# One step of a gated-conv and mixture-of-experts decoder on one core: one expert's load, the tiles' last order, and a second load queue

## The reference, cut to what matters

```python
x = x + jnp.concatenate([z_a, z_b], axis=-1) @ w_out
x = x + _hier_moe(_rmsnorm(x, g_ffn), ...)     # the top 2 of 8 experts in the best of 4 groups
...
for e in range(N_EXPERTS):                      # 32
    hid = jax.nn.silu(t @ w_gate[e]) * (t @ w_up[e])
    out = out + combine[:, e:e + 1] * (hid @ w_down[e])
...
y_prompt = _rmsnorm(xp, g_final)
y_sample = _rmsnorm(xs, g_final)
```

## Time and profile before

| what | us |
|---|---|
| median of 3 runs (lowest, highest) | 535.75 (534.46, 538.24) |
| the profiled execution, its own time | 540.91 |
| its span | 539.0 |
| TensorE busy | 483.3 (90%) |
| VectorE, ScalarE, GpSimd busy | 237.7, 100.4, 183.3 |
| DMA | 141.25 MB, mean 262 GB/s |
| chain that ended last: TensorE, DMA, VectorE, issue, SP's queue | 71%, 12%, 5%, 5%, 3% |

### The profile page before, as it was taken

How to read it: one execution, slowest core, us unless ns; L and a number is a source line. 1 busy time by engine, 2 the same in 40 slices (tenths; PEclk the granted TensorE clock), 3 DMA queues, 4 the chain that set the end, 5 groups by cost and what they waited for, 6 DMA issues and landing times.

```text
span 539.0 us, 8928 instructions
## 1 busy us (share of the span) xinstructions
PE 483.3 (90%) x3301; PEld 285.3 (53%) x3302; DVE 237.7 (44%) x514; ACT 100.4 (19%) x204; POOL 183.3 (34%) x282
## 2 busy tenths in 40 slices
PE   6999999999999999999679998989898982998884
PEld 3787777777777545545334443444443441443331
DVE  4219999999964422245821222222122210221246
ACT  5131011002104423324301111101111110011223
POOL 3010817647394600111234443333443332234101
PEclk9989999999999999999789999999999996999999
DMA  8995006100000597023959799999999999999477
GB/s 328 310 391 142 0 2 258 54 2 0 1 1 1 189 412 315 39 69 124 403 192 420 284 411 422 402 397 421 419 418 419 417 419 420 420 418 421 195 272 256
DMA packets 35509, 141.25 MB, mean 262 GB/s; under 512 B 10080, under 2 KB 10096, under 8 KB 23193
## 3 DMA queue, kind: packets, MB, share of 16 engines
q1 hardware_dynamic: 29194, 127.91, 60.4%
q0 software_dynamic: 4960, 9.45, 4.7%
q10 hardware_dynamic: 1327, 3.49, 1.8%
HBM read 134.47 MB, written 13.17 MB: 274 GB/s over the span
## 4 chain that ended last, share of the span: by engine, by line
PE 71%; DMA 12%; DVE 5%; issue 5%; SPq 3%; ACT 2%; POOL 1%; DVEq 0%; POOLq 0%; ACTq 0%
PE bank L1284 26%; PE bank L1367 10%; PE bank L1485 9%; PE bank L1505 8%; PE bank L1480 8%; DMA region_x<-in_w_up 5%; DMA region_w<-in_w_in 3%; PE bank L1277 2%; DMA slot<-y_rows 2%; SPq L402 2%; PE bank L1495 2%; PE bank L1433 1%; DVE ua L1169 1%; PE bank L1393 1%; DVE ua L1171 1%
## 5 line engine op out<-in xcount | busy, mean ns | idle before, releaser
L1284 PE MATMUL bank<-region_h,region_w 128*128 128x256 f32 (+1 forms) x576 | 142.3, 409 | 0.0
L1284 PEld LDWEIGHTS bank<-region_h,region_w 128*128 128x128 f32 x576 | 110.2, 192 | 30.5 <-issue 0.8
L1169 DVE TENSOR_TENSOR ua<-ua,bank 128x128 f32<-128x128 f32 x30 | 8.7, 288 | 174.2 <-ACT ua L639 174.2
L1367 PE MATMUL bank<-region_w,z 128*128 128x512 f32 x128 | 56.7, 596 | 0.2 <-ACT z L584 0.2
L1505 PE MATMUL bank<-region_w,ua 128*32 128x512 f32 x328 | 50.3, 598 | 3.3 <-DVE ua L1171 3.3
L928 DVE SCALAR_TENSOR_TENSOR z<-ub,par,z 128x512 f32<-128x512 f32 x60 | 48.7, 812 | 0.0
L928 DVE SCALAR_TENSOR_TENSOR region_x<-ub,par,region_x 128x512 f32<-128x512 f32 x56 | 45.9, 820 | 0.0
L1485 PE MATMUL bank<-region_w,z 128*32 128x256 f32 x512 | 45.1, 403 | 0.2 <-issue 0.2
L792 POOL COPY gcol<-gidx 128x1 uint32 (+1 forms) x30 | 5.4, 180 | 108.9 <-DVE sb_rows L1158 108.9
L723 POOL TENSOR_TENSOR ub<-region_x 128x512 f32<-128x512 f32 x4 | 20.2, 5056 | 63.8 <-ACT ub L538 32.6
L1485 PE MATMUL bank<-slot,z 128*32 128x256 f32 x192 | 25.9, 425 | 14.5 <-DMA region_w<-in_w_up 9.9
(11 more groups left out here) (244 smaller groups left out, 647.5 us busy)
## 6 DMA issues: line engine op xcount, KB each, us to landing
region_w<-in_w_down SPq DMA_DIRECT2D x21, 1024.0 KB
region_w<-in_w_gate SPq DMA_DIRECT2D x16, 1024.0 KB
region_w<-in_w_up SPq DMA_DIRECT2D x16, 1024.0 KB, 15.7
region_w<-in_w_in SPq DMA_DIRECT2D x4, 2048.0 KB, 19.5
slot<-in_w_gate SPq DMA_DIRECT2D x6, 1024.0 KB, 14.8
slot<-in_w_up SPq DMA_DIRECT2D x6, 1024.0 KB
slot<-in_w_down SPq DMA_DIRECT2D x6, 1024.0 KB
region_x<-in_w_up SPq DMA_DIRECT2D x5, 1024.0 KB
```

The costliest lines, as they stand in the source:

```text
L1284: ins = mm(ps[2 * bank + j][:, 0:LEN[j]], sec[name][:, k, c * P:(c + 1) * P], hT[:, k, CUT[j]], start=(k == 0), stop=(k == KC - 1))
L1367: ins = mm(ps[2 * (t % 2) + j][0:n, :], z[:, k, t * P:t * P + n], w_out_sb[:, k, j * 512:(j + 1) * 512], start=(k == order[0]), stop=(k == ...
```

## The change

Three edits. Place 4's three loads move from behind the wait for the normalized rows to behind the first gather (SP's wait for those rows moves along), ahead of place 5's last part. The order in which tiles are finished changes from 0, 2, 1, 4, 3 to 0, 4, 2, 1, 3: loads, additions, norms, roots and stores follow, and the counts of the waits with them (`SUMMED` is 0, 4, 2). And the y of k = 1 of tiles 0 and 1 (`BY_ACT`) is loaded from ScalarE's queue, behind waits of its own for the last scatters and one small activation; SP issues the other eight.

```diff
+BY_ACT = (0, 1)
-FINISH = (0, 2, 1, 4, 3)
+FINISH = (0, 4, 2, 1, 3)
+SUMMED = tuple(t for t in FINISH if t not in BY_PE)
...
             load_expert(3, 3)
-            sp.wait_ge(s_h2, NT)
-            load_part(4, 0, 4)
-            load_part(4, 1, 4)
-            load_part(4, 2, 4)
             for i in range(2):
                 sp.wait_ge(s_h2d[i], 16 * ((NT + 1 - i) // 2))
             sp.wait_ge(s_x1t, 2 * NT)
+            sp.wait_ge(s_h2, NT)
             sp.wait_ge(s_gath[0], 16)
+            load_expert(4, 4)
             load_part(5, 0, 5)
             sp.wait_ge(s_tab, 1)
...
-            for t, k in ((0, 0), (0, 1), (2, 0), (1, 0), (2, 1), (1, 1), (4, 0), (4, 1), (3, 0), (3, 1)):
+            for t, k in ((0, 0), (4, 0), (4, 1), (1, 0), (2, 0), (2, 1), (3, 0), (3, 1)):
                 sp.dma_start(yg[k][t][0:TROWS[t], :], y_dram[k * NTOK + t * P:k * NTOK + t * P + TROWS[t], :])\
                   .then_inc(s_yg[k][t], 16)
...
+            act.wait_ge(s_ysc[1], pairs * 16)
+            act.wait_ge(s_ysc[0], (pairs + odd) * 16)
+            nc.scalar.activation(small[:, 63:64], eps_rms, ACT.Sqrt)
+            for t in BY_ACT:
+                act.dma_start(yg[1][t][:, :], y_dram[NTOK + t * P:NTOK + (t + 1) * P, :]).then_inc(s_yg[1][t], 16)
             for at, t in enumerate(FINISH):
...
-                act.wait_ge(s_fin, t // 2 + 1)
+                act.wait_ge(s_fin, SUMMED.index(t) + 1)
...
-                    dve.wait_ge(s_fin1, t // 2 + 1)
+                    dve.wait_ge(s_fin1, SUMMED.index(t) + 1)
...
             add_row(0, 0)
             add_row(0, 1)
+            add_row(4, 0)
+            normed(0)
+            add_row(4, 1)
             add_row(2, 0)
-            normed(0)
+            normed(4)
             add_row(2, 1)
-            add_row(4, 0)
-            normed(2)
-            add_row(4, 1)
-            for t in (1, 4, 3):
+            for t in (2, 1, 3):
                 normed(t)
```

## The result

The changed kernel took 542.18 us (median of 4 runs, 539.76 to 543.01) against 535.9 of before (4 runs, 534.46 to 538.24, three of them those shown above): a ratio of 1.0078, 95% interval 1.0047 to 1.011. (Ratios here are worked out from all the runs, and differ a little from the quotient of the two medians, which is 1.012 in this case.) Forecast were 535.0 and a range up to 538.7, so the forecast was wrong, and on the wrong side. Two repeats, each with 12 runs beside 35 of before, gave 1.0024 (0.9998 to 1.005) and 1.0005 (0.9976 to 1.0034).

What follows compares the result with a forecast made beforehand. From 306 us the expert weight stream was taken to set the pace, then the tail after the last scatter. Stream -2.4 plus tail +1.7 gave -0.7: 540.91 to 540.2, less the carried 5.2, 535.0 us; range 532.0 to 538.7.

Steps and rivals of the forecast that it cites:

- I take 3.0: First gather with idle engines: takes 3.0 us instead of 4.77, so it lands 1.8 us earlier.
- I expect the clock not to drop: TensorE's first block: fillers lead straight into it, so its first 62 matmuls take 3.87 us instead of 5.23, 1.4 more gained.
- TensorE leads by 3.2 us after its first block: Start of the blocks: the earlier gather (1.8) and the kept clock (1.4) put TensorE 3.2 us ahead.
- the lesser of 2.4 and TensorE's lead: Weight stream: moved loads fill idle engine time, reaching the state of 306 us 2.4 us earlier; gain taken as 2.4.
- I carry the difference over: Total: the profiled execution ran 5.2 us above the runs' median, and the forecast subtracts the same 5.2 from 540.2.
- rival B: Gather isn't helped or the lead is lost in the stream, while ScalarE's order costs 1.7 us: 537.45, chance 0.2.
- part 1: Place 4's matrices loaded behind the first gather: gain 2.4 us, bounds nothing to 2.9.
- I cost the second queue at zero: Tail y loads: a second queue only saves issue time, 5 us of issue against 16 us to the last landing; effect zero.
- ScalarE's row of three tiles takes the place of the last landing as the bound: Tail: ScalarE works through tiles 2, 1 and 3 in a row, making the tail 1.7 us longer.
- A: Rival: the tail is free, through earlier landings for tile 2 or a short GpSimd operation: 533.3, chance 0.15.
- C: Rival: tile 4's half-speed packets slow the other queue's full tiles beside them, 1.05 us on top: 536.1, chance 0.1.
- D: Rival: interleaving is no hindrance, other ports stay filled, 1 MB moves at 420, 1.05 us less: 534.0, chance 0.1.

Runs made afterwards that it cites:

- b0: The kernel before, unchanged, run and profiled again: 537.78 us, ratio 0.9995 to before.
- a0: The changed kernel run again without any diff: ratio 1.0024 to before.
- p1_move: Before with only the move of place 4's three loads behind the first gather: ratio 0.9983 to before.
- d1: The changed kernel without the second queue, all ten y loads on SP in order 0, 4, 1, 2, 3: ratio 0.9975 to before.
- p2_order: Before with only the tile order changed to 0, 4, 2, 1, 3, all ten y loads on SP: ratio 1.0005 to before.
- a1: The changed kernel with 50 instead of 32 fillers ahead of tile 1's first y: ratio 1.001 to before.
- p3_queue: Before, in its own tile order, with only the second y of tiles 0 and 1 loaded from ScalarE's queue: ratio 1.0016 to before.
- c1_t1first: a1 with tile 1 finished ahead of tile 2 (order 0, 4, 1, 2, 3), same loads: ratio 0.9999 to before.
- d0: The changed kernel run once more without any diff, in the last session: ratio 1.0005 to before.
- a2: The changed kernel with tile 1's first y issued second on SP's queue instead of fourth: ratio 1.004 to before.
- d3: Before with only place 4's down matrix moved behind the first gather, keeping 24 fillers: ratio 0.9968 to before.
- c4_split18: Before with only place 4's down matrix moved behind the first gather, and 18 instead of 24 fillers: ratio 0.9972 to before.

## Why the prediction was wrong

**The gather and the clock: right as read, wrong as a gain.** "I take 3.0" for the gather: measured 3.1, and 2.99 to 3.66 in all nine other profiles with all three loads moved, against 4.1 to 4.9 in the five profiles that moved none. "I expect the clock not to drop": so it was, 3.87 us. But in b0 the clock doesn't drop either, and the chain goes through fillers that end 5.2 us after the gather's issue. The step that failed is "TensorE leads by 3.2 us after its first block". Against b0 the lead is 0.1 us (5.62 to 5.70), and 1.2 where the fillers run at the upper clock (4.53 in a0). It was a lead over the one execution of before, among five, whose fillers were short (5.35 us) and ran out ahead of the gather.

**The stream: the arithmetic held, and the lesser of two terms was wrong.** The rule was "the lesser of 2.4 and TensorE's lead". With the lead at about 0 the gain is about 0, and p1_move measures 0.9983 (0.995 to 1.0016), no change that can be told from none. I had computed the lead from the profile of before alone and had filled the 11.0 us of idle engines without asking how much of it was due to TensorE being 2 us late in that very execution. In b0 place 2 is freed at 31.8 us, not 33.5, and by +36 us its engines have moved 16.98 MB, where the ten profiles with the move have 16.3 to 17.1.

**"I carry the difference over."** In the total this is the largest error, and it hid the other. The profiled execution was 5.2 us above the median, and I took these 5.2 us for a constant spread that the change can't touch. 2.1 of them sat between the gather and the first y load (245.52 against 243.44), the stretch in which the gain was computed. With them taken out, the forecast's own terms would have given about 0 + 1.7, that is rival B: 537.45. Term by term: the changed kernel's profiled execution took 541.58 us against the 540.2 of the sum, 1.4 more (part 1 gave 1.1 instead of 2.4, the tail cost 2.4 instead of 1.7, the start was 0.5 shorter), but its runs have a median of 542.18, above the profiled one and not 5.2 below it. These 5.8 us are most of the miss of 7.2.

**The tail: a number near the forecast, by another path.** Forecast +1.7, measured +2.4 in the two profiles. Tile 2's second addition ended 16.3 us after the last scatter's landing, exactly as summed: its first y landed 12.0 us after the first issue, as the sum had it, and GpSimd's first operation took 0.89 instead of 1.17. But the 16.3 are 17.3 in a0, where all landings came some 1 us later, so the exact match is partly luck. What failed:

- "I cost the second queue at zero." In the new order it is the queue that costs: d1 without it ends 1.6 to 1.9 us sooner than the three profiles of the changed kernel and has before's length within its spread (25.34; 24.0 to 25.9). Of these 1.8, 1.9 and 1.6 us, tile 2's second addition ending later makes 0.6, 1.5 and 0.7, and TensorE 1.2, 0.3 and 0.9. The last landing didn't move: it came 15.9 us after the first issue in both profiles (530.1 - 514.24; 528.5 - 512.65), and over all profiles at 15.2 to 17.0 with one queue and 15.3 to 16.8 with two. By the Trainium skill ("DMA: Bandwidth & Descriptors", section Issuing engines are not separate DMA queues) queues of any engine interleave on the same 16 engines; the trace agrees. I had asked only after the last landing. Three loads interleaved at the front make the first ones late: the first addition starts 5.1, 6.0 and 5.2 us after the first issue in the three profiles of the changed kernel and 4.6 to 6.1 in all nine with two queues, against 3.6 to 3.8 in the nine profiles with one. What sets the place in that range isn't shown.
- "ScalarE's row of three tiles takes the place of the last landing as the bound", as the whole cause: the new order alone costs about 0.5 us (p2_order 25.10, d1_moveorder 25.34, against 24.7 in the mean of seven), less than executions differ by. Its chain is longer, 17.7 us from first addition to last product (a1) against at most 16.7 (p3_queue, c1_t1first), but with one queue the first addition starts early enough to hide most of it: 3.6 + 18.4 = 22.0 in p2_order, where tile 2's landing still comes in between, against 22.1 in b0. The step after that landing was even cheaper than summed, 6.6 us from the end of tile 2's second addition to the last product instead of 7.15. Before's order has slack for a late start and the new one has not; this is why the two together cost more than either alone.
- TensorE was not in the sum at all. Tile 1's first y, fourth on SP's queue and behind ScalarE's two, lands so late that TensorE idles 4.1 us, its granted clock falls to 0.50 and its row of 16 matmuls takes 9.96 us. That holds tile 3 back by 1.13 us (0.81 in d0). Taken away (a1), the end came no sooner, since the first addition began 6.1 us after the first issue in that execution, 5.1 in the first profile. c1 shows the price of the order on the other path: 1.1 us of its 2.2.

**Rivals.** B is the nearest: the lead is lost and the tail costs, 0.7 more than its 1.7. But its reason for the tail, ScalarE's row alone, is not what cost, and it stood at 0.2. A, C and D didn't happen: A's early landing of tile 2 was refuted by 16.3 us, and against C and D the last landing stayed where the sum had it. The total of 537.45 that B gives would lie 0.3% above the median; the repeats have 0.24% and 0.05%. What made the first session show 0.78% stays partly open. Its four runs of the changed kernel had a mean granted clock of 0.964, where those of a0 and d0_again have 0.973, and in its profile gather to first y took 244.43 us instead of 243.13 and 243.50. That is 1 us of the further 3. The other side moved too: the four runs of before have a median of 535.9, and in the four sessions of 35 runs before's is 537.66 to 539.13, while the changed kernel's 542.18 became 539.80 and 539.51. Four runs on each side were too few.

## What to carry to other kernels

Before a gain is taken from one profile, ask whether the stretch in which it lies is typical: where the profiled execution stands above the median, part of that distance may be the very stall that the change is to remove, and then it is neither gained nor carried over. A second queue for loads that share engines leaves the last landing and makes the first one later, so weigh it by the first use too, above all where the work behind that use is a chain of two engines without slack. And idle transfer time filled behind an event gives nothing if the same bytes leave the time ahead of it empty; whether moving only what fits (one matrix of three here) gives more is not shown by these runs.

## What was not expected of the hardware

- The same 24 fillers took 5.35 us where the granted clock was 1.00 throughout (the first profile of before, a0, a2, d0, d3) and 6.9 to 8.0 in the ten other profiles, where it was at 0.50 for the first of them (b0, the changed kernel's first profile, a1) or fell on the way (p1_move: 0.75, then 0.50, in windows of 2 us from the first filler on). What TensorE did just before was alike: ten small matmuls with pauses of 0.7 and 0.8 us between them. In the 2 us ahead of the fillers the clock was already at 0.50 in b0 and a1, and at 1.00 in a0 and p1_move; what set it isn't shown. These 1.6 us decide whether an earlier gather is of use at all, and they differ between executions of one kernel (the changed kernel: 6.92 in the first profile, 5.35 in a0).
- The first gather took 4.1 to 4.9 us where three loads of 1 MiB were issued 8 us ahead of it, and 3.0 to 3.7 where none was, in one execution of each kernel. With two of the three ahead of it (the split) it took 4.9, 3.2 and 3.4. The 4.9 were in c4_split18, where the engines moved 0 GB/s from 266 to 268, around its issue at 266.49. So full engines are not the whole of it.
